# Sixty expert pairs spread differently over the mixer's marks of a hybrid decoder layer

## The reference, cut to what matters

```
proj = x @ w_in                                   # attention q,k,v; DeltaNet q,k,v,z; beta, decay
att  = sliding-window attention (window 128), rotary positions, sinks
dn   = gated DeltaNet, chunks of 64, short convolution of 4 taps, state carried over tokens
x1   = LayerNorm(alpha*x + concat(att, dn) @ w_out)
q    = x1 @ w_query ; s = q . sub_keys            # 16 lists of 128 scores a token
top 16 of each list -> 16x16 sums per head -> top 16 -> 128 experts a token
h    = gelu(x1 . u[expert]) * softmax(best)       # u, v: rows of 1024 floats
x2   = LayerNorm(alpha*x1 + sum h * v[expert])
```

## Time and profile before

| what | value |
|---|---|
| median of three runs | 3605.18 us |
| profiled execution: its own time / its span | 3588.42 us / 3586.6 us |
| mean granted TensorE clock | 0.836 of full |
| TensorE / VectorE / ScalarE / GpSimd busy | 69% / 62% / 32% / 33% |
| gathers (q0): bytes, share of the 16 DMA engines | 1073.81 MB, 75.0% |
| weights (q1): bytes, share | 172.66 MB, 12.0% |
| mean DMA rate over the span | 350 GB/s |

### The profile page before, as it was taken

How to read it: one execution, slowest core, us unless ns; L and a number is a source line. 1 busy time by engine, 2 the same in 40 slices (tenths; PEclk the granted TensorE clock), 3 DMA queues, 4 the chain that set the end, 5 groups by cost and what they waited for, 6 DMA issues and landing times.

```text
span 3586.6 us, 41030 instructions
## 1 busy us (share of the span) xinstructions
PE 2474.1 (69%) x11840; PEld 1363.2 (38%) x11840; DVE 2209.2 (62%) x5469; ACT 1132.0 (32%) x3475; POOL 1169.5 (33%) x1028
## 2 busy tenths in 40 slices
PE   7757775777667777577756776677765777665554
PEld 6554342444335333254423533334432444321111
DVE  4285657665674757756486565775567574775444
ACT  3115321353223532235312442234322353222222
POOL 0013423333332433424323242332433233333443
PEclk9779987888879988799878997878987899787777
DMA  6039999899998999989989899989999899998997
GB/s 279 24 147 354 400 369 363 346 337 366 390 369 344 359 386 370 381 325 385 363 359 378 328 395 356 364 342 350 397 371 366 343 365 384 363 356 355 420 420 329
DMA packets 174953, 1254.90 MB, mean 350 GB/s; under 512 B 20184, under 2 KB 20312, under 8 KB 23520
## 3 DMA queue, kind: packets, MB, share of 16 engines
q0 software_dynamic: 147456, 1073.81, 75.0%
q1 hardware_dynamic: 25056, 172.66, 12.0%
q10 hardware_dynamic: 2176, 5.36, 0.4%
HBM read 1247.56 MB, written 4.19 MB: 349 GB/s over the span
## 4 chain that ended last, share of the span: by engine, by line
PE 32%; DVE 27%; DMA 19%; issue 12%; ACT 8%; POOL 1%; DVEq 0%; POOLq 0%; ACTq 0%; SPq 0%
DMA ring<-in_uv,expert_used 17%; PE expert_sum L720 14%; DVE ring L1340 9%; PE bank L475 6%; PE bank L483 6%; DMA chunk<-in_weights 3%; ACT diag L938 2%; DVE arena L1066 2%; PE bank L489 2%; ACT h_raw L934 1%; DVE arena L1075 1%; DVE arena L1080 1%; DVE arena L1073 1%; PE bank L504 1%; DVE conv L1089 1%
## 5 line engine op out<-in xcount | busy, mean ns | idle before, releaser
L436 POOL DMA_INDIRECT ring<-in_uv,expert_used x1024 | 1169.3, 1142 | 2386.8 <-PE expert_sum L720 1986.2
L720 PE MATMUL expert_sum<-ring,diag 128*64 128x512 f32 x4096 | 1256.1, 749 | 968.3 <-ACT diag L938 968.2
L1340 DVE CUSTOM_DVE_ANT_0 ring<-ring,x_pair 128x1024 f32<-128x1024 f32 x1024 | 1216.8, 1222 | 482.6 <-DMA ring<-in_uv,expert_used 467.6
L720 PEld LDWEIGHTS expert_sum<-ring,diag 128*64 128x64 f32 x4096 | 305.7, 162 | 1698.8 <-ACT diag L938 1031.6
L931 ACT ACTIVATE h_raw<-h_raw 128x2 f32<-128x2 f32 x512 | 104.1, 203 | 1615.5 <-DVE h_raw L1340 1614.8
L483 PE MATMUL bank<-oT,chunk 128*128 128x128 f32 x3008 | 362.5, 283 | 28.2 <-DMA chunk<-in_weights 27.5
L483 PEld LDWEIGHTS bank<-oT,chunk 128*128 128x128 f32 x3008 | 353.5, 198 | 74.4 <-issue 39.7
L938 ACT ACTIVATE diag<-const,h_raw 128x64 f32<-128x64 f32 x1024 | 300.2, 339 | 3.4 <-PE expert_sum L720 1.7
L934 ACT ACTIVATE h_raw<-h_raw,gate_used 128x1 f32<-128x1 f32 x1024 | 245.6, 286 | 16.7
L1089 DVE SCALAR_TENSOR_TENSOR conv<-conv_in,conv_w,conv 128x128 f32<-128x128 f32 x288 | 80.4, 346 | 188.2 <-ACT conv L779 188.2
L1066 DVE MAX8 arena<-arena 128x8 f32<-128x128 f32 (+1 forms) x384 | 104.1, 327 | 124.9 <-ACT arena L911 110.3
(11 more groups left out here) (229 smaller groups left out, 2189.5 us busy)
## 6 DMA issues: line engine op xcount, KB each, us to landing
chunk<-in_weights SPq DMA_DIRECT2D x137, 1024.0 KB, 8.8
ring<-in_uv,expert_used POOLq DMA_INDIRECT x1024, 10.4
ring<-in_weights SPq DMA_DIRECT2D x15, 1024.0 KB, 20.5
oT<-in_xT SPq DMA_DIRECT2D x8, 512.0 KB, 7.9
kept<-in_weights SPq DMA_DIRECT2D x4, 1024.0 KB, 11.8
x<-in_x SPq DMA_DIRECT2D x8, 512.0 KB, 6.6
out<-o_cat ACTq DMA_DIRECT2D x8, 512.0 KB, 5.3
sub_keys<-in_sub_keys ACTq DMA_DIRECT2D x1, 1024.0 KB
```

Source lines behind the costliest of these rows:

```text
L436: pool.indirect_dma_start(out=ring[:, (j % RING) * 2 * D:(j % RING + 1) * 2 * D], out_offset=None, in_=io["uv"], in_offset=bass.IndirectOf ...
L720: mm = pe.matmul(expert_sum[i][c * SPAN:(c + 1) * SPAN, :], diag[:, (j % DIAGS) * SPAN:(j % DIAGS + 1) * SPAN], ring3[:, j % RING, D + i * ...
L1340: dve.tensor_tensor_reduce(u, u, x_pair[:, (j % 2) * D:(j % 2 + 1) * D], 1.0, 0.0, ALU.mult, ALU.add, h_raw[:, j:j + 1]).then_inc(dotted.s ...
```

## The change

Only the table `STEPS` changes. The sum at the marks stays 60, the mixer's instructions, the gathers and their order stay as they are; each pair stands at another place between the mixer's instructions on TensorE, ScalarE and VectorE.

```diff
 STEPS = dict(
-    q=1, kv=1, conv_q=1, turn_qk=1, conv_k=1, conv_v=1, z=1, scores=1, softmax=1, turn_p=1, att_o=2,
+    q=1, kv=1, conv_q=2, turn_qk=1, conv_k=2, conv_v=2, z=1, scores=1, softmax=1, turn_p=1, att_o=2,
     norms=1, decay=1, kk=1, aT=1, pow2=1, pow4=1, pow8=1, prod3=1, turn32=1, merge32=1, turn64=1,
-    merge64=1, solve=1, ws0=1, kv0=1, ws1=1, kv1=1, dn=1, o_T=1, out0=3, out1=2, x1_T=2, qu0=2,
-    top0=1, sel0=0, pick0=1, qu1=2, top1=1, sel1=2, pick1=0, qu2=2, top2=0, sel2=2, pick2=3, qu3=2,
-    top3=1, sel3=2, pick3=1,
+    merge64=1, solve=1, ws0=1, kv0=1, ws1=1, kv1=1, dn=1, o_T=1, out0=2, out1=2, x1_T=1, qu0=2,
+    top0=1, sel0=1, pick0=1, qu1=1, top1=1, sel1=1, pick1=1, qu2=1, top2=1, sel2=1, pick2=1, qu3=1,
+    top3=2, sel3=2, pick3=3,
 )
```

## The result

The change makes the kernel slower, by 0.7%. Twenty runs of each gave medians of 3606.6 us before and 3636.0 us after, ratio 1.0074 (95% interval 1.0055 to 1.0092). The forecast was 3584 us, faster than before, and the range ended at 3626.

What follows compares the result with a forecast made beforehand. The prediction took mixed waits as the bound: transfers in the merges, the mixer elsewhere. Terms +6 - 6.6 - 10.5 + 8 = -3.1 us a round, seven rounds -22 us from 3605.2, gave 3584 us; range 3550 to 3626.

Steps and rivals of the forecast that it cites:

- What bounds the kernel: Whole round: mostly the mixer sets the pace, transfers only in the merges; some 59 us of DMA time per round unused.
- late chunks: Rival, chance 0.23: refills delay the in-projection's weight chunks, scores 12 us late, round +2.9, time 3625.
- The end stretch: From the fourth top-k to the next round, 11 pairs instead of 8: +8 us a round, bounds 0 and +15.
- in-projection: Round's start, three pairs more by `conv_v` (9 instead of 6): z and scores later, +6 us, bounds +1 and +15.
- gives back most of the three pairs: Fourth top-k onward: the ring of four pairs, full at its start, offsets most of the three pairs added there.
- the upper bound was +15: Fourth top-k to the next round: the most the added pairs could cost, three pairs at full transfer time.
- The signs of being wrong: Forecast wrong if scores are over 9 us late, a top-k period exceeds 35 us, or the end exceeds 79 us.
- The step with the transposes: At `conv_q`, q/k transposes fall behind an ADD waiting for its diagonal; `conv_k`'s chunks start 3.3 us later.
- no further cost comes behind the scores: From `scores` to `ws1`: same requests 6 us later, the saturated stretch starts and ends 6 us later, nothing added.
- first come, first served: Rejected transfer order in the in-projection: 11 transfers ahead of or with the z chunk, shift 8 to 9 us.
- The top-k periods: First three, 12 pairs instead of 16: TensorE ends each at 31.9 us, 95.6 instead of 106.1, -10.5 us.
- The out-projection: Two pairs fewer at `out0` and `x1_T`: first top-k starts sooner, -6.6 us, bounds -3.9 and -15.6.

## Why the prediction was wrong

*What bounds the kernel, and the shape of the answer* were right: a win or loss of idle DMA time, stretch by stretch, with all four signs. The sum of small terms of both signs was -3.1 with errors of +2.5, +0.7, +1.9 and +3.7, all one way, and these turned a gain into a loss. The largest single rival on the slow side, late chunks, was the wrong mechanism: without the chunk transfers the shift at the scores stays 7.0.

*The end stretch, forecast +8, is the step that failed.* It measured +11.7, and +13.0 by itself. It is not enough alone to turn the sign: with +8 there the round would still be 2.0 us longer, and the in-projection below has most of the rest. I followed the order of ADDs correctly to the last issue (+8.3 for +8.5), then took the landing to come as soon behind it as before the change, 7.5 us. It came 11.1 us behind it, and 8.2 before. The order of issue was priced and the queue of transfers was not. I had +8 us, 2.7 us a pair, for a place where three pairs brought in cost 4.3 each (13.0) and three taken out gave 4.9 each (14.6). That the ring, full at the start, "gives back most of the three pairs" was wrong: half of the six gathers were given back, and 4 us of idle DMA time before pair 57 took half of that away again. That the upper bound was +15 stood in the text; the value taken should have been nearer to it, for the share of 0.95 in the earlier trace rows says that this stretch has hardly any idle transfer time to give.

*The signs of being wrong stayed silent.* Scores came 7.4 us late (limit 9), no period passed 35 us, and the end was 76.6 us after the fourth maxima, where the forecast had 76 and the limit was 79. But the 76 was 68.0 + 8, on a base that was 2.9 us too long (65.1). Two errors cancelled there: that the end came to "about 76 us" was luck.

*The in-projection, forecast +6, measured +8.5 at the state update* (+7.4 at the scores, +8.0 at the merges). The step with the transposes was right and makes half of it (3.7 less with them ahead): `conv_k`'s chunks start 3.4 us late, and 3.3 was forecast. What was missing comes behind: z starts 6.0 us late where the working had 5.0, and ends 7.4 late. The working held the waits for chunks as they were and had one longer wait for a diagonal; the runs showed 1.2 us less of the former and 3.5 us more of the latter. That no further cost comes behind the scores was not quite right either, 1.1 us more.

On the sharing of DMA time, the Trainium skill (DMA: Bandwidth & Descriptors, Queues, rings and completion order) has an engine take turns between its queues. The chunks in the stretch up to the scores landed in 9.9 us instead of 7.8:

```profile
chunk<-in_weights SPq DMA_DIRECT2D x7, 1024.0 KB, 9.9
```

That agrees with a shared rate. In the kernel before, a gather issued at 1472.2 landed at 1484.2, ahead of a chunk issued at 1470.8 that landed at 1487.3. So first come, first served was rejected rightly, and late chunks cost next to nothing up to the scores.

*The top-k periods, forecast 31.9 each*, measured 32.5, 31.7, 32.8, in the order of TensorE that was worked out. Their starts in the round shown:

```profile
1389.65 0.87 DVE L1066 MAX8 arena<-arena 128x8 f32<-128x128 f32 x4 [4.67 <-ACT arena L911]
...
1422.02 0.88 DVE L1066 MAX8 arena<-arena 128x8 f32<-128x128 f32 x4 [6.94 <-ACT arena L911]
...
1453.63 0.87 DVE L1066 MAX8 arena<-arena 128x8 f32<-128x128 f32 x4 [6.19 <-ACT arena L911]
```

Each waits for ScalarE's copy, as forecast. The three are 97.0 us together for 95.6, a small miss. The larger one, as I read it and no run shows apart, is what the saving was worth: twelve pairs at 348 GB/s leave idle DMA time behind that the end must make up. *The out-projection* measured -5.9 for -6.6; its terms, added up, put the first top-k at 1362.0 and not at the 1362.5 written.

The profiled execution before was a quick one (18 us under its median), and I carried a difference over, so this had no part in the error of the time.

## What to carry to other kernels

Price moved work by the resource that is saturated at its new place, and by the free time at its old one: here a pair costs 4 to 5 us where DMA is busy, and 2 to 3 us where an engine orders the work. Where an issue is late and its queue is full, price the landing and not only the issue. When several small terms of both signs make the sum, take the one with the widest bounds and ask which end its rows are nearer to. Check the base of a sign of being wrong as well as its change. And keep moved work off the path to what the next stage waits for: one more pair at `pick2`, ahead of the query chunks, made a period 10 us longer, its own ADD included. That, pairs taken out of the end, and the in-projection's pairs put behind the transposes gave 3.5%.

## What the runs showed of the hardware

How long TensorE stood still did not by itself tell whether the granted clock fell behind it. In the changed kernel it fell to the lower level (a mean of 0.65 over the next 2.8 us) behind waits of 3.68 and 3.69 us. In the kernel before it fell behind two waits of 2.46 us, and stayed at 1.00 behind one of 2.52 us and one of 3.50 us at the earlier trace rows. In the changed kernel a 1 MB gather issued while no other transfer was on its way landed in 5.5 to 7.8 us. With the queue full one landed every 2.5 us, and each took 7 to 11 us from issue to landing in the end stretch. A stop of GpSimd of 10.1 us with four gathers and a chunk still on their way cost the DMA engines about 4 us.
